# First queries and keys of three attention branches made in the gate stage and placed from SBUF

## The chip, the cores and the metric

One NeuronCore of a Trainium2 chip runs the whole kernel in one launch. The metric is the device time of that launch in microseconds. The engines are TensorE (PE, matmuls and transposes), VectorE (DVE), ScalarE (ACT), GpSimd (POOL) and SyncE (SP, which here only issues DMAs). Each works its own list in order; semaphores order them against each other.

## What is computed

A decoder layer on 1024 tokens of width 1024, in float32. Four causal attention branches work on one input projection; what the change touches is the order of their parts.

```python
def token_mixer(x, w_in, b_forget, sinks, w_branch, w_gate, b_gate, w_out):
    (aq, ak, av, bq, bk, bv, cq, ck, cv, ciq, cik, ciw, dq, dk, dv, df) = split(x @ w_in)
    o_a = banded_attention(aq, ak, av, slopes_a, 127, 1, sinks)     # 8 heads on 2 key heads
    o_b = dilated_attention(bq, bk, bv, slopes_b)                   # 8 heads
    o_c = dsa_attention(cq, ck, cv, ciq, cik, ciw, slopes_c, 256)   # 8 heads on 1 key head, 256 best keys
    o_d = forgetting_attention(dq, dk, dv, df + b_forget)           # 8 heads
    proj = einsum('bsnk,nkd->bsnd', stack(o_a, o_b, o_c, o_d), w_branch)
    gates = sigmoid(x @ w_gate + b_gate)
    return sum(gates * proj, axis=2) @ w_out

def reference(...):
    x = layer_norm(ALPHA * x + token_mixer(x, ...))
    return layer_norm(ALPHA * x + conv_glu_ffn(x, ...))
```

In branch C each query sees the 256 keys of highest index score; where scores are equal, the earlier keys win.

## The kernel before

Every float32 product is made of three matmuls: operands are split into a high part (rounded to a format that TensorE takes at full rate) and a low part (the rest), and hi x hi, lo x hi and hi x lo are summed. ScalarE writes the high part, GpSimd (of weights) or VectorE (of activations) the low part. The list of steps is: transposes of x, the index projections, the index scores, the **gate stage**, then for each branch in the order B, D, A, C: its first q and k projection, its v projection, attention in four pairs of heads, and the **merge** (branch projection and gating), and last the output projection and the feed-forward part.

Gate stage (`GATE_PRODUCTS`, L1225). Of the 32 gate tiles of 128 channels, 22 are made here, two per round, in 11 rounds (`NGATE`). A round takes seven products of 2x2 blocks (of 12 matmuls each) where two plain projections take 96 matmuls. ScalarE and GpSimd make the operands, VectorE combines the products, ScalarE applies the sigmoid, and SP stores the tiles in DRAM (`gates_dram`). Between them VectorE works at the search for the 256th best score of each query (`topk_search`, L2399; 191 steps, up to 14 a round).

Between branches (steps `q`, `k` or `kv_c`). PE runs whole projections of 48 matmuls (L911) into a PSUM pair; ScalarE (`q_hi`, `k_hi`, L1675) and VectorE (`q_lo` L2519, `k_lo` through `lo_part` L2648) place them in `heads`, from PSUM: queries scaled, with the low part below the high one; keys twice, on both halves of the partitions. `heads[:, 0:4]` also holds the operand of the merge before (`o_hi`). Then PE starts v; after 30 matmuls it makes the first scores (L972, L973), and it goes on to the filler (the next pair's projections, L927) only after VectorE has copied v out of PSUM (L2889). In branch C, v comes by transposes of the k/v projection (L963). `biased` (L2504) adds the distance bias and takes the row minimum, ScalarE makes the exponentials (L1777), VectorE the reciprocals (L2514), GpSimd the normalised probabilities (L2230).

Merge. PE makes eight tiles of 24 matmuls (L1247 to L1271) in four PSUM places; `gated` on VectorE (L2957) multiplies each by its gate, and in D and A a second operation (L2962) adds it to the running sum. Tile t+4 waits for the gating of tile t. ScalarE and GpSimd split the next weights meanwhile (L1652, L2175), two tiles ahead; the last of these splits waits for the merge's last tile, and both engines do it before they go on to the next branch. Of B's merge, four tiles of the sum are spilled to DRAM and come back later (`spill`).

Equal scores (`topk_distances`, L2441 to L2456): per 128 queries six steps on VectorE, 36 in all, which turn scores into distances. They and the last steps of the search run beside the merges and the projections between branches (`topk_parts`).

SP issues all loads of weights in the order of the steps, two raw tiles deep. Before branch D it also loads the forget biases of heads 0 and 1 (`forget_bias`, L1511) over the tiles that hold B's bias and the distances. It waits there for the semaphore `bias_used`, which VectorE raises once B's bias and its own use of these tiles are done. `forget_bias(0)` and `(1)` stand right after the load of D's v weights, and the weights of D's second pair behind them.

## Time and profile before

| | us |
|---|---|
| median of 3 runs (lowest, highest) | 2093.43 (2091.26, 2094.61) |
| the profiled execution | 2093.97 |
| its span, first to last instruction | 2092.2 |
| PE busy | 2060.4 (98%) |
| DVE busy | 1536.4 (73%) |
| ACT busy | 968.5 (46%) |
| POOL busy | 937.3 (45%) |

In a profile a group is named by line, engine and operation, then what it writes and reads (`out<-in`) by the program's names. "Idle before" is the time for which the engine stood before the instruction, with what ended it behind an arrow. Matmuls overlap in the records: one of 512 columns is shown with 0.39 us, but the next starts 0.23 us after it. So the distance of starts counts, and PE shown as busy is not PE without loss. A timeline gives start, duration, engine, line and operation; rows in sequence are merged with their count.

### The profile page before, as it was taken

What the parts mean: (1) busy time and instruction counts of PE and PEld (TensorE: products, weight loads), DVE (VectorE), ACT (ScalarE), POOL (GpSimd) and SP (SyncE); (2) the same over time, 40 slices, a digit from 0 to 9 for tenths busy, and PEclk for the clock granted to TensorE, in tenths of its full rate; (3) what the DMA queues carried; (4) which work ended last, traced back from release to release, by engine and by line L of the source; (5) the groups of instructions that cost most, each with busy time, mean ns of one, the idle gap of its engine ahead of it and who ended that gap; (6) DMA issues with size and microseconds to landing.
All of it is one profiled execution on the core that took longest, in us unless ns stands there. A gap on an engine that the chain in (4) does not pass through costs nothing.

```text
span 2092.2 us, 28999 instructions
## 1 busy us (share of the span) xinstructions
PE 2060.4 (98%) x10382; PEld 1727.0 (83%) x10382; DVE 1536.4 (73%) x2549; ACT 968.5 (46%) x1740; POOL 937.3 (45%) x796
## 2 busy tenths in 40 slices
PE   9999999999999999999999999999999999999998
PEld 7788888888888888888888888888788888888887
DVE  8678887777686666797785666668877777775668
ACT  5543334566615556615635666523433333344540
POOL 4287752333322223324523333524756565645651
PEclk9999999999999999999999999999999999999999
DMA  4233323110042111230031000441566665558862
GB/s 132 72 111 110 101 91 62 31 31 21 26 152 64 50 32 51 75 100 28 22 121 31 21 21 11 141 161 61 180 181 203 191 192 161 171 189 310 270 215 92
DMA packets 197373, 224.26 MB, mean 107 GB/s; under 512 B 25704, under 2 KB 149608, under 8 KB 197232
## 3 DMA queue, kind: packets, MB, share of 16 engines
q1 hardware_dynamic: 194320, 212.43, 32.7%
q10 hardware_dynamic: 2912, 10.00, 1.3%
q8 instruction: 83, 1.36, 0.3%
q14 instruction: 58, 0.48, 0.1%
HBM read 164.17 MB, written 58.23 MB: 106 GB/s over the span
## 4 chain that ended last, share of the span: by engine, by line
PE 87%; DVE 7%; issue 2%; ACT 2%; POOL 1%; DMA 0%; DVEq 0%; ACTq 0%; POOLq 0%
PE pair L1359 13%; PE pair L927 13%; PE pair L911 7%; PE pair L1225 7%; PE obank L1359 5%; PE pair L1388 5%; PE obank L1021 4%; PE chunk L1000 4%; PE pair L1318 3%; PE chunk L1388 3%; PE obank L1225 3%; PE pair L972 3%; PE pair L973 3%; PE pair L1271 2%; PE obank L1388 2%
## 5 line engine op out<-in xcount | busy, mean ns | idle before, releaser
L2175 POOL TENSOR_TENSOR w_lo<-w_raw,w_hi 128x1024 fp32r<-128x1024 f32 x64 | 159.5, 2492 | 311.1 <-ACT w_hi L1652 311.0
L1675 ACT ACTIVATE pt_hi<-chunk 128x512 fp32r<-128x512 f32 (+1 forms) x272 | 150.8, 555 | 179.2 <-PE chunk L1000 177.8
L2578 DVE TENSOR_TENSOR pt_lo<-chunk,pt_hi 128x512 fp32r<-128x512 f32 (+1 forms) x272 | 173.2, 638 | 80.1 <-ACT pt_hi L1675 75.7
L2230 POOL TENSOR_SCALAR prob<-prob,att 128x256 f32<-128x256 f32 (+4 forms) x172 | 118.1, 696 | 198.5 <-DVE att L2514 198.2
L927 PE MATMUL pair<-act_hi,w_hi 128*128 128x512 f32 x432 | 186.4, 432 | 2.5 <-DVE heads L2519 2.3
L927 PE MATMUL pair<-act_hi,w_lo 128*128 128x512 f32 x432 | 170.0, 393 | 0.0
L927 PE MATMUL pair<-act_lo,w_hi 128*128 128x512 f32 x432 | 169.4, 392 | 0.0
L2399 DVE TENSOR_SCALAR_CACHE_REDUCE o_top<-score,stat 128x384 uint8<-128x384 f32 (+1 forms) x186 | 167.0, 941 | 0.5
L1021 PE MATMUL obank<-pt_hi,heads 128*128 128x256 f32 (+1 forms) x568 | 148.4, 285 | 0.6 <-DVE pt_lo L2578 0.6
L1777 ACT ACTIVATE prob<-prob,att 128x257 f32<-128x257 f32 (+6 forms) x172 | 120.5, 702 | 39.3 <-DVE att L2504 38.0
L1021 PE MATMUL obank<-pt_lo,heads 128*128 128x256 f32 (+1 forms) x568 | 138.6, 281 | 0.0
L972 PE MATMUL pair<-heads 128*128 128x512 f32 (+3 forms) x352 | 119.9, 347 | 5.7 <-DVE att L2504 4.8
L911 PE MATMUL pair<-act_hi,w_hi 128*128 128x512 f32 x288 | 116.8, 405 | 5.0 <-DVE act_lo L2648 2.7
L1652 ACT ACTIVATE w_hi<-w_raw 128x1024 fp32r<-128x1024 f32 x64 | 67.4, 1053 | 111.8 <-PE obank L1271 38.3
L1000 PE MATMUL chunk<-ident,prob 128*128 128x128 f32 x660 | 111.9, 274 | 2.7 <-DVE pt_lo L2578 2.1
L1021 PEld LDWEIGHTS obank<-pt_lo,heads 128*128 128x128 f32 x568 | 108.2, 190 | 6.8
L1021 PEld LDWEIGHTS obank<-pt_hi,heads 128*128 128x128 f32 x568 | 107.4, 189 | 7.7 <-DVE pt_lo L2578 1.1
L973 PE MATMUL pair<-heads 128*128 128x512 f32 (+3 forms) x352 | 113.1, 334 | 0.0
L911 PE MATMUL pair<-act_lo,w_hi 128*128 128x512 f32 x288 | 112.6, 391 | 0.0
L911 PE MATMUL pair<-act_hi,w_lo 128*128 128x512 f32 x288 | 111.0, 392 | 0.0
L2230 POOL TENSOR_SCALAR mid<-mid,att 128x384 f32<-128x384 f32 (+4 forms) x56 | 37.8, 683 | 162.4 <-DVE att L2514 162.4
L927 PEld LDWEIGHTS pair<-act_hi,w_lo 128*128 128x128 f32 x432 | 81.1, 188 | 18.6
(489 smaller groups left out, 5932.5 us busy)
## 6 DMA issues: line engine op xcount, KB each, us to landing
down_sums<-dn_sums SPq DMA_DIRECT2D x40, 512.0 KB, 6.4
w_raw<-in_w_in SPq DMA_DIRECT2D x37, 512.0 KB, 3.8
gates<-o_t SPq DMA_DIRECT2D x22, 512.0 KB, 2.9
up_raw<-in_w_up SPq DMA_DIRECT2D x22, 512.0 KB, 4.8
gate_raw<-in_w_ffn_gate SPq DMA_DIRECT2D x22, 512.0 KB, 6.0
hidden<-gelu_s SPq DMA_DIRECT2D x22, 512.0 KB, 3.3
dn_raw<-down_sums SPq DMA_DIRECT2D x44, 256.0 KB, 4.1
h_in<-down_sums SPq DMA_DIRECT2D x44, 256.0 KB, 4.8
```

The costliest lines, as they stand in the source:

```text
L911: last = nc.tensor.matmul(dst[0:cols, s:s + HALF], w[:, k, :], a[:, k, s:s + HALF], start=(i == 0), stop=(i == len(order) - 1))
L927: last = nc.tensor.matmul(pair[1][:, s:s + HALF], w[:, k, :], a[:, k, s:s + HALF], start=(k == 0 and n == 0), stop=(k == NKT - 1 and n == 2))
L972: nc.tensor.matmul(dst[:, s:s + m], q, k_hi[:, s:s + m], start=True, stop=False)
L973: last = nc.tensor.matmul(dst[:, s:s + m], q, k_lo[:, s:s + m], start=False, stop=not masked)
L1000: last = nc.tensor.transpose(t[:, at:at + P], prob_slot(br, 2 * j + w)[:, s:s + P], ident[:])
L1021: last = nc.tensor.matmul(obank[bank_of(br)[j] % 2][:, q0:q0 + width], v, part[:, slot, at:at + width], start=(c == 0 and b == 0 and w == ...
L1225: last = nc.tensor.matmul(place, w[:, tokens_of(k)], gate_tokens(p, part, k), start=(p in (1, 6, 5) and k == 0 and m == 0), stop=(k == 3 a ...
L1359: last = nc.tensor.matmul(dst, w[:, cols], moving, start=(p in (1, 6, 5) and k == 0 and m == 0), stop=(k == 3 and m == 2), skip_group_chec ...
L1388: last = nc.tensor.matmul(banks[t], l[:, t * P:(t + 1) * P], r, start=(p in (6, 1, 5, 3) and k == 0 and m == 0), stop=(k == KFF - 1 and m ...
L2175: nc.gpsimd.tensor_tensor(split_into(1, g), w_raw[:, g % 2, 0:kt * cols], split_into(0, g).bitcast(F32), ALU.subtract).then_inc(lo_ready, 1)
L2399: nc.vector.tensor_scalar(junk[:, b % 2, 0:(i + 1) * P], s, limit if isinstance(limit, float) else limit[:, b:b + 1], None, ALU.is_ge, ALU ...
L2578: nc.vector.tensor_tensor(pt_lo[:, n % PT_SLOTS, 0:m], t[:, 0:m], pt_hi[:, n % PT_SLOTS, 0:m].bitcast(F32), ALU.subtract).then_inc(chunk_f ...
```

## The change

The first q and k of branches D, A and C (in C the shared k/v) are no longer projected between branches. They are six more tiles of the gate stage, which grows from 11 to 14 rounds; ScalarE writes them with a copy in place of the sigmoid, and SP stores them in DRAM (`heads_dram`). SP loads them during the merge before the branch into `o_t[:, 0]` and `o_t[:, 1]`, once tile 4 of that merge is free to be gated (`load_heads`). A new step `heads` places them from there in parts, counted by `first_placed`: the first half of the first head, the second half, and the other head. On VectorE the gating of the merge's last tile moves behind the first of these parts; ScalarE spills B's last tile behind the second. The search is now done within the gate stage. Of the equal-score steps, four rows of blocks run beside B's merge, four steps a tile, before the signal `bias_used`; the other two rows run beside D's merge.

```diff
+HEAD_TILES = [(what, br) for br in BRANCH_ORDER[1:] for what in ("q", "k")]
+GATE_TILES = [(br, dt) for br in BRANCH_ORDER for dt in STORED_GATES[br] if (br, dt) not in FILLER_GATES] + HEAD_TILES
...
-        if br == C:
-            out += [("kv_c",)]
-        if br == A:
-            out += [("k", A, 0)]
-        out += [("q", br, 0)]
-        if br in (B, D):
-            out += [("k", br, 0)]
+        out += [("q", br, 0), ("k", br, 0)] if br == B else [("heads", br)]
         out += [("v_c",)] if br == C else [("v", br, 0)]
...
+                    if step[1] != B:
+                        pe.wait_ge(first_placed, placed_first(step[1], 1))
                     scores(step[1], step[2], 0)
...
+            def load_heads(br):
+
+                at = BRANCH_ORDER.index(br) - 1
+                if at == 0:
+                    sp.wait_ge(merge_free, 4)
+                else:
+                    sp.wait_ge(sum_done, sums_of(BRANCH_ORDER[at]) + 4)
+                for what in ("q", "k"):
+                    tile = GATE_TILES.index((what, br))
+                    sp.wait_ge(gate_stored[tile % 2], 16 * (tile // 2 + 1))
+                    sp.dma_start(first_head(what), tile_kept((what, br))).then_inc(heads_loaded, 16)
...
+            def first_heads(br):                                   # ScalarE
+
+                at = BRANCH_ORDER.index(br)
+                act.wait_ge(merge_full, NKT * at)
+                act.wait_ge(heads_loaded, 32 * at)
+                first_half(br, 0)
...
+            def other_heads(br):
+
+                first_half(br, 1)
+                if br == D:
+                    act.wait_ge(merge_free, merge_at(B) + NKT)
+                    spill(NKT - 1)
+                q_hi(br, 0, 1, first_head("q")[HD:P, :])
+                if br != C:
+                    k_hi(1, first_head("k")[HD:P, :])
...
+            def first_half(br, s):                                 # VectorE
+
+                q_lo(br, 0, 0, first_head("q")[0:HD, half_cols(s)], half_cols(s))
+                k_lo(0, first_head("k")[0:HD, half_cols(s)], cols=half_cols(s)).then_inc(first_placed, 1)
+
+            def first_heads(br):
+
+                before = BRANCH_ORDER[BRANCH_ORDER.index(br) - 1]
+                first_half(br, 0)
+                gated(before, NKT - 1)
+                dve.wait_ge(merge_free, merge_at(before) + NKT)
+                if before != B:
+                    dve.wait_ge(sum_done, sums_of(before) + NKT)
...
                 elif kind == "v":
+                    if step[1] != B:
+                        first_half(step[1], 1)
+                    biased(step[1], step[2], 0)
+                    if step[1] != B:
+                        other_head(step[1])
+                    biased(step[1], step[2], 1)
+                    inverse(step[1], 0)
                     if step[1] == D:
                         dve.wait_ge(mid_stored, 16 * len(SPILLED))
-                    if step[1] == A:
-                        topk_parts((SEARCH_PARTS - topk_done.n) % DISTANCE_PARTS)
-                    for u in range(2):
-                        biased(step[1], step[2], u)
-                    inverse(step[1], 0)
...
                 if (br, pr) == (C, 0):
                     biased(br, pr, 0)
                     biased(br, pr, 1)
+                    first_half(br, 1)
+                    other_head(br)
                     inverse(br, 0)
...
-                    topk_parts(start_parts)
-                    for dt in range(NKT):
+                    if br == D:
+                        topk_parts(LATE_DISTANCES)
+                    elif br == A:
+                        own(nc.vector.tensor_copy(dist_a[:], dist[:, SEQ - 2 * P:SEQ]))
+                    for dt in range(NKT if br == FINAL else NKT - 1):
...
+                        if br == B and dt < ROWS_BESIDE:
+                            topk_parts(EARLY_ROWS * DISTANCE_PARTS // ROWS_BESIDE)
+                            if dt == ROWS_BESIDE - 1:
+                                signal().then_inc(bias_used, 2)
```

The two engines' own marks behind `def first_heads` and `def first_half` are added here for the reader.

## Rows read from the trace of the kernel before

**Rows 1.** The page's first part: busy time of PE.
```profile
PE 2060.4 (98%) x10382; PEld 1727.0 (83%) x10382; DVE 1536.4 (73%) x2549; ACT 968.5 (46%) x1740; POOL 937.3 (45%) x796
```

**Rows 2.** Busy us (count): PE, PEld, DVE, ACT, POOL; gate stage, B's merge.
```profile
105.00:314.00 209.00, 209.00 (x923) 173.06 (x923) 178.30 (x426) 77.82 (x121) 151.09 (x118) 1.00 0.34 104
...
572.00:615.00 43.00, 43.00 (x191) 35.45 (x191) 36.00 (x71) 9.10 (x10) 9.65 (x4) 1.00 0.56 183
```

**Rows 3.** Timeline of PE: merge ends, and starts of what waits.
```profile
615.41 0.39 PE L911 MATMUL pair<-act_hi,w_hi 128*128 128x512 f32 x1
...
650.93 0.50 PE L927 MATMUL pair<-act_hi,w_hi 128*128 128x512 f32 x1
...
920.68 0.39 PE L911 MATMUL pair<-act_hi,w_hi 128*128 128x512 f32 x1
...
955.29 0.49 PE L927 MATMUL pair<-act_hi,w_hi 128*128 128x512 f32 x1
...
1098.10 0.39 PE L911 MATMUL pair<-act_hi,w_hi 128*128 128x512 f32 x1
...
1127.39 0.50 PE L972 MATMUL pair<-heads 128*128 128x512 f32 x1 [0.76 <-DVE att L2504]
```

**Rows 4.** Timelines of DVE, ACT and POOL at the end of B's merge.
```profile
615.68 1.23 DVE L2957 TENSOR_TENSOR mid<-obank,prob 128x1024 f32<-128x1024 f32 x1 [0.69 <-PE obank L1271]
...
615.67 1.06 ACT L1652 ACTIVATE w_hi<-w_raw 128x1024 fp32r<-128x1024 f32 x1 [9.82 <-PE obank L1271]
...
616.81 2.41 POOL L2175 TENSOR_TENSOR w_lo<-w_raw,w_hi 128x1024 fp32r<-128x1024 f32 x1 [8.48 <-ACT w_hi L1652]
```

**Rows 5.** Placement of half heads (timelines), of whole ones from SBUF (tile heads).
```profile
668.78 1.38 DVE L2648 SCALAR_TENSOR_TENSOR heads<-pair,heads 64x512 fp32r<-64x512 f32 x2 [0.80 <-ACT heads L1675]
...
667.49 1.19 ACT L1675 ACTIVATE heads<-pair 64x512 fp32r<-64x512 f32 x2
...
L2648 DVE SCALAR_TENSOR_TENSOR heads<-mid,heads x12: 1216/1220/1223, 398.0 to 827.8; 64x1024 fp32r<-64x1024 f32 x12
```

**Rows 6.** Timelines of DVE and POOL: sums at the end of D's merge.
```profile
917.50 1.22 DVE L2962 SCALAR_TENSOR_TENSOR mid<-mid,prob 128x1024 f32<-128x1024 f32 x1
...
922.31 3.25 DVE L2962 SCALAR_TENSOR_TENSOR mid<-mid,prob 128x1024 f32<-128x1024 f32 x1
...
922.08 2.40 POOL L2175 TENSOR_TENSOR w_lo<-w_raw,w_hi 128x1024 fp32r<-128x1024 f32 x1 [8.48 <-ACT w_hi L1652]
```

**Rows 7.** Timelines of ACT and DVE at first scores, D and C.
```profile
648.66 0.51 ACT L1777 ACTIVATE prob<-prob,att 128x256 f32<-128x256 f32 x1 [2.59 <-DVE att L2504]
...
649.65 1.23 DVE L2889 COPY mid<-pair 128x1024 f32<-128x1024 f32 x1 [0.18 <-PE pair L911]
...
1123.70 0.76 DVE L2648 SCALAR_TENSOR_TENSOR heads<-chunk,heads 128x256 fp32r<-128x256 f32 x2
1124.49 0.29 DVE L2504 CUSTOM_DVE_ANT_0 prob<-pair,dist_a 128x128 f32<-128x128 f32 x1
...
1126.18 0.54 DVE L2504 CUSTOM_DVE_ANT_0 aux<-pair,score 128x384 f32<-128x384 f32 x1
```

**Rows 8.** SP: timeline, waits by cause (570 to 640), DMA issues (626 to 627).
```profile
625.34 0.81 SPq L1511 DMA_DIRECT2D aux<-c_forget  x2
626.19 6.20 SPq L1410 DMA_DIRECT2D w_raw<-in_w_in  x2
...
SPq L1510 <- DVE stat L2356: 16.5, 1, 16.5
...
w_raw<-in_w_in SPq DMA_DIRECT2D x1, 512.0 KB, 6.1
```

**Rows 9.** Timeline of DVE: gating of B's tile 5, equal-score steps of 768.
```profile
604.80 1.23 DVE L2957 TENSOR_TENSOR mid<-chunk,o_t 128x1024 f32<-128x1024 f32 x1 [0.69 <-PE chunk L1271]
...
930.07 1.76 DVE L2448 TENSOR_TENSOR_SCAN aux<-prob 128x768 f32<-128x768 f32 x1
931.86 1.02 DVE L2452 SCALAR_TENSOR_TENSOR prob<-aux,stat,prob 128x768 f32<-128x768 f32 x1
```

More of the change, by code:

```diff
@@ L794, in gate_bias_of, with tile_weights, tile_kept, first_head @@
             return gate_bias[:, br * NKT + dt:br * NKT + dt + 1]
+        def tile_weights(tile):
+            if tile not in HEAD_TILES:
+                return w_tile(w_gate[0], tile[0] * D_MODEL + tile[1] * P, P)
+            what, br = tile
+            return w_tile(w_in[0], Q_COL[br] if what == "q" else CK if br == C else K_COL[br], P)
+        def tile_kept(tile):
+            return heads_dram[HEAD_TILES.index(tile)] if tile in HEAD_TILES else gates_dram[tile]
+        def first_head(what):
+            return o_t[:, 0 if what == "q" else 1, :]
+        def placed_first(br, part):
+            return 3 * (BRANCH_ORDER.index(br) - 1) + part
         gate_out = [o_t[:, 2, :], o_t[:, 3, :]]
@@ L1518, in _ @@
                                  allow_slow_non_contiguous=True).then_inc(late_params, 16)
+                if step[0] == "heads":
+                    load_heads(step[1])
                 for n, source in enumerate(ring_sources(step)):
@@ L2795, in _ @@
                     dve.wait_ge(consts_ready, 1)
-                if kind == "kv_c":
-                    topk_parts(10 ** 6)
-                    own(nc.vector.tensor_copy(dist_a[:], dist[:, SEQ - 2 * P:SEQ]))
                 if kind == "x":
@@ L2832, in _ @@
                         counted(9)
-                    topk_parts(TOPK_FIRST.get(step[:2], 0))
-                    if step == ("q", D, 0):
-                        dve.wait_ge(pair_free[0], tiles[0].n)
-                        signal().then_inc(bias_used, 2)
                     k = step[1] in (B, D)
```

200 lines of the change are left out of this document (102 added, 98 removed).

## The prediction, made before the change was run

> **What bounds the kernel now.** I read the page first: TensorE (PE) is busy for 2060.4 of 2092.2 us [rows 1]. Then I read the stretches by stage: in the gate stage PE is busy for all 209.00 us while it starts 923 matmuls, which makes 0.2264 us a matmul of 512 columns; VectorE (DVE) has 178.30 us of work there, and in the merge of branch B 36.00 of 43 us [rows 2]. So PE sets the end as long as its operands arrive, and a change is worth what it takes from PE's list less what PE then has to wait. Last I read the three places where one branch ends and the next begins. The reader is to see there where PE starts the first removed projection, and where it starts the work that can't begin before the vector engine has caught up [rows 3].
>
> The profiled execution took 2093.97 us (span 2092.2), the median of the three runs is 2093.43. I make the sum against 2093.97 and take off the half microsecond at the end.
>
> **What PE loses and gains in work.** Six projections go from between the branches: q and k of D, k and q of A, the shared k/v and q of C. Each is 8 k-tiles x 2 halves x 3 parts = 48 matmuls, together 288, or 65.3 us at 0.2267 us (209.4 us over the stage's own 924). Three rounds come to the gate stage, each 7 products x 12 = 84 matmuls, together 252, or 57.1 us. The rounds there so far leave PE no idle time [rows 2]; VectorE does 14 search steps a round there before and after, so I give the new rounds the same pace. All search steps (14 rounds x 14 - 2 = 194 places for 191 steps) now fit in the stage; before, 39 of them ran between the branches, beside PE work that covered them, so taking them from there gives PE nothing. Net: **-8.2 us**.
>
> **What covered the turn from branch to branch, and no longer does.** At each turn 96 matmuls, 21.8 us of PE work, disappear. Under them VectorE did its last gating, ScalarE (ACT) and VectorE placed q and k, and ScalarE split the next weights. Now PE has only the v projection (or, in the turn to C, eight transposes and 12 matmuls) while all of this follows in one chain after the merge's last matmul. Let e be that end: VectorE and ScalarE start within 0.1 us of it, so e is 615.6 for B to D, 920.9 for D to A, 1098.3 for A to C [rows 3, 4].
>
> The chain, from rows: ScalarE first splits a weight tile (1.06 us), and GpSimd (POOL) starts its 2.4 us low part at e+1.2 [rows 4]. ScalarE then places the first half of one head: three activations of 64x512, two of which took 1.19 [rows 5]; the first is there at about e+1.75. VectorE's partner ops (half width 0.69 each, full width 1.22 [rows 5]) read their source from SBUF now, and the subtracted part too, where the removed ones read PSUM. The nearest rows say what that means beside GpSimd: the same kind of op with both inputs in SBUF took 1.22 us alone and 3.25 when GpSimd had begun a 2.40 us split just before; it ended 1.1 us after GpSimd did [rows 6]. So VectorE's first placement waits for e+3.6. The bounds are e+1.75 (no blocking) and e+3.6; I take the latter, since the conditions are those of the slow row.
>
> The Trainium skill, page SBUF — State Buffer, section "Who interferes with whom", has this as a rule: a VectorE instruction with two SBUF inputs contends with a GpSimd instruction that reads SBUF, and whoever starts first has the shared ports for the whole instruction. The row of 3.25 us agrees. By the rule and by the row the wait is the same 1.85 us at each turn; it speaks against reading the first heads from SBUF.
>
> **D to A.** VectorE: three half ops to e+5.7; the gating of the last tile and its sum, 1.2 each, to e+8.2; second half of the first head to e+10.3; the first scores' softmax start 0.4; the other head, three full ops, to e+14.4; the second start 0.5; exp 0.6 and reciprocal 0.2; copy of v 1.23 [rows 7], to e+17.1. PE's filler can't begin before this copy, as before, where it began at 955.29 right behind it. Before, less the 21.8 us removed, is 933.5; now 938.05. **Loss 4.5 us.** GpSimd's six tiny sink ops and two bias ops may add up to 1 us by the same ports.
>
> **B to D.** The same chain without the sum, with shorter score ops: copy done and filler begun at e+15.65 = 631.3 against 650.93 - 21.77 = 629.2, a loss of 2.1. The last tile's spill (an issue from ScalarE's queue, moved behind the second half of the first head) costs nothing: the second head's VectorE ops come later anyhow. But here a moved step has a second effect. SyncE (SP), after the v weights, waits for bias_used before it sends two loads of forget biases, and only behind them the next weights (k of the second pair). Those are the very tile that ScalarE now splits at e, ahead of every placement; before, that place had k of the first pair, loaded long ago. SyncE stands in this wait for 16.5 us in the trace, and its weight load, sent behind the two bias loads, landed 6.1 us after its issue [rows 8]. The signal now comes after VectorE's steps beside tile 5 of merge B. Tile 5 is gated from 604.8 for 1.2 us; then four steps of the 768-wide row, 1.76 + three of about 1.02 [rows 9], make 610.8, and 613.0 if the scan meets GpSimd's split. Add 0.85 to the issue and 6.1 to the landing [rows 8]: the weights are there at 620.0, 4.3 us after ScalarE wanted them; without the port effect 618. PE, which wants the first placed heads 30 matmuls (6.8 us) into v, then stands. **Loss 2.1 + 4.3 = 6.4 us**, bounds 0.2 and 8.
>
> **A to C.** PE's cover is 1 us of transposes and 2.7 of filler. VectorE: first half to e+5.7, gating and sum to e+8.2, v's low parts 0.76, two score ops 0.65 (0.29 and a wider one) [rows 7], second half 2.1, other q 1.2, reciprocal, two more score ops 1.15 (0.54 in the row and the next wider), to e+14.2. Unit 4 of the scores waits for these, as it did at 1127.39. Now 1112.5 against 1127.39 - 21.77 = 1105.6. **Loss 6.9 us**, bounds 5.0 (no blocking) and 8.
>
> **Edits at nothing.** The copies in place of sigmoids for the six tiles take the same slot on ScalarE. Six stores of 512 KB go out in the gate stage as the 22 others do, six loads come during merges with some 20 us to land. The equal-score steps in merge B just fit: the 768-wide row's six steps are those 4.8 us and two of about 0.8, and the rows of 384, 512 and 640 scaled from it bring the four to some 20 us, with 7.3 for six gatings, in the 32.6 us that PE takes for six tiles; PE's v needs the gating of tile 6 done, by my sum at 614.3 against 615.4; should they be late by 2 us, 1 us is lost. Five steps at merge D's start run before the first tile is ready or delay it within PE's four places.
>
> **Sum.** -8.2 + 6.4 + 4.5 + 6.9 = +9.6 us: 2103.6, against the median 2103.1.
>
> **Rivals.**
> The forget-bias wait is hidden (the steps finish early, or the load lands faster): B to D loses 2.1 only, sum +5.3, 2099.3. Against it: the loads in order behind one another [rows 8].
> GpSimd doesn't block (it splits later, or VectorE gets in first): the turns cost 2.7 + 2.7 + 5.0, sum +2.2, 2096.2; with the bias wait gone too, 0.2 + 2.7 + 5.0 - 8.2, 2093.7: **no change**. This decides from losses under 12.4 us on. For it speaks that only one kind of op is seen blocked; against it the start times.
> **Faster**: the placement runs under v, and PE keeps its saving: 2085.8 at most. It decides where the three losses stay under 4 us together. For it: PE's waits on placement are small today. Against: my shortest chain for C alone loses 5.
> Worse than forecast: more port conflicts and merge B's steps late, 2107 to 2109.
> That the change doesn't do what it says: the new gate rounds stretch to VectorE's pace. It is busy 85% there; I leave this in the worse case.
>
> **How the numbers follow.** Forecast 0.45, hidden bias wait 0.15, worse 0.05: slower 0.65. No blocking, with or without the bias wait: 0.20. Faster 0.15. Bounds of 0.2% (4.2 us) are about what a measurement of this kernel can tell from no change. The range has its upper end from C and B to D at 8 and A at 5.5 (+13.3, 2107), its lower end 2091, so that it takes in all of no change and leaves most of faster out.
>
> **What the profile will show.** PE's idle time: some 6 us before unit 4 of C, up to 4 us before the first placed scores of D and more before the first transposes of probabilities in D and A. Placement ops on VectorE of 2 us and more at each turn where GpSimd runs. A weight split on ScalarE at 620, not 615.7, of the turn to D (all moved by 57 us), released by a DMA. The gate stage 266.5 us long without a gap. I'm wrong if PE shows under 4 us of waits at the three turns together, or if PE's losses sit in the gate stage.

## The result, and the profile after

The changed kernel took 2113.46 us, the median of five runs (2112.66 to 2114.48), against 2093.43 before: a ratio of 1.0097, with a 95% interval of 1.0082 to 1.0111. It is slower by 20 us. The forecast was slower, but at 2103.1, with a range that ended at 2107: the direction was right and the size half of what came. All medians here are of executions at nearly full clock (0.99 and more); one execution of one kernel below, e8_spread, took 3782.84 us at a granted clock of 0.80 and is left out.

The profiled execution of the changed kernel took 2112.66 us (span 2110.8), 18.7 more than that of before. The page's first line on PE answers [rows 1]: fewer matmuls and less busy time, in a longer span. So the time is in PE's waits and not in its work.

```profile
span 2110.8 us, 29071 instructions
PE 2058.3 (98%) x10346; PEld 1724.3 (82%) x10346; DVE 1547.6 (73%) x2572; ACT 983.0 (47%) x1776; POOL 962.9 (46%) x823
```

The next view answers [rows 2]: busy time and count of PE, PEld, DVE, ACT and POOL, then the granted clock and the DMA share, in the gate stage (some 57 us longer than before), and in the merge of B.

```profile
105.00:371.30 266.30, 266.30 (x1176) 220.50 (x1176) 228.10 (x545) 98.18 (x154) 193.19 (x151) 1.00 0.35 106
...
630.00:673.00 43.00, 42.77 (x189) 34.96 (x187) 38.00 (x47) 8.29 (x9) 10.31 (x4) 1.00 0.53 183
```

PE is busy for all of the gate stage. To see where the rest went, the timeline of PE is read at the edges of the merges, here of the changed kernel: first matmul of merge B and of merge D, first matmuls behind merge D, first of merge A, first work behind merge A, first of the last merge.

```profile
628.97 0.44 PE L1264 MATMUL pair<-heads,w_hi 128*128 128x512 f32 x1
...
924.27 0.45 PE L1264 MATMUL pair<-heads,w_hi 128*128 128x512 f32 x1
...
969.79 0.39 PE L925 MATMUL pair<-act_lo,w_hi 128*128 128x512 f32 x1
...
1088.16 0.44 PE L1264 MATMUL pair<-heads,w_hi 128*128 128x512 f32 x1
...
1132.13 0.38 PE L977 MATMUL chunk<-ident,o_t 128*128 128x128 f32 x2
...
1330.57 0.45 PE L1264 MATMUL pair<-heads,w_hi 128*128 128x512 f32 x1
```

In the table a stretch runs from one such edge to the next (the last matmul of a merge where it says end). "Due" is the stretch before, less the 21.77 us of projections that left it; the loss is what the changed kernel took beyond that.

| stretch | before | due | after | loss | predicted |
|---|---|---|---|---|---|
| up to the start of merge B | 571.78 | 628.9 (+57.1) | 628.97 | 0.1 | 0 |
| start of merge B to start of D's | 304.93 | 283.16 | 295.31 | 12.15 | 6.4 |
| merge D | 43.75 | 43.75 | 45.06 | 1.31 | 0 |
| end of merge D to start of A's | 133.69 | 111.92 | 118.83 | 6.91 | 4.5 |
| end of merge A to start of the last | 213.62 | 191.85 | 198.67 | 6.82 | 6.9 |
| the rest | 780.68 | 780.68 | 780.21 | -0.5 | 0 |

Merge A takes 43.73 us in both. Added up: 57.2 - 65.3 + 12.15 + 1.31 + 6.91 + 6.82 - 0.5 = +18.6 us, the difference of the two spans. The three turns lose 25.9 us where 17.8 were forecast, and merge D loses 1.3 that were not.

What PE waited for, by cause (total, times, longest), first at the turn to D (670 to 700), then from merge D over the turn to A (924 to 1000), then at the turn to C (1131 to 1150):

```profile
PE pair L986 <- DVE heads L2705: 5.6, 1, 5.6
PE pair L925 <- DVE mid L2858: 3.2, 1, 3.2
PE chunk L1014 <- POOL prob L2282: 0.8, 1, 0.8
...
PE pair L986 <- DVE att L2559: 3.7, 1, 3.7
PE pair L1288 <- issue: 1.4, 1, 1.4
PE chunk L1014 <- POOL prob L2282: 1.0, 1, 1.0
...
PE pair L986 <- DVE att L2559: 4.8, 2, 2.9
PE pair L986 <- DVE heads L2705: 2.0, 1, 2.0
```

The waits at the turn to C make 6.8 us (before the change PE waited 1.2 us there, 0.4 and the 0.76 of [rows 3]). At the turn to D they make 9.6 of 12.15, at the turn to A 4.7 of 6.91. Besides, the granted clock is at half (1.2 of 2.4 GHz) for 6.8 us from 687.8, from 984.8 and from 1138.4. This is the turn to A, 6.8 us at half and the 10 us behind them:

```profile
984.80:991.60 6.80, 5.60 (x17) 4.53 (x18) 2.82 (x9) 2.52 (x8) 1.15 (x4) 0.50 0.00 0
991.60:1001.60 10.00, 10.00 (x63) 8.81 (x63) 6.02 (x21) 4.99 (x16) 3.77 (x13) 1.00 0.00 0
```

What the half clock costs depends on where it lies. While VectorE works through its chain, a slower PE only waits less afterwards. So each turn is divided where PE can't go on before VectorE has caught up: at the start of the filler in D and A, at the scores of unit 4 in C (1146.69, below). VectorE's copy of v in D, and the first filler matmul of D and of A:

```profile
697.20 1.22 DVE L2980 COPY mid<-pair 128x1024 f32<-128x1024 f32 x1
...
698.56 0.47 PE L941 MATMUL pair<-act_hi,w_hi 128*128 128x512 f32 x1
...
987.35 0.78 PE L941 MATMUL pair<-act_hi,w_hi 128*128 128x512 f32 x1
```

Measured from the last matmul of the merge, with 21.77 us taken off before, the turns to D, A and C lose 12.2, 4.9 and 7.0 us up to this point, and -0.1, 2.0 and -0.2 us behind it. In D and C the half clock ends ahead of this point. VectorE works there with no gap of more than 0.1 us, from 684.75 to 696.4 and from 1134.0 to 1146.5, so the half clock costs nothing. In A it goes on for 4.3 us behind the filler's start, where PE has no wait that it didn't have before, and it is what the 2.0 us are.

**The turn to D.** In merge B, VectorE never stands still after the first tile, and it is late. Its timeline (starts, durations), with GpSimd's three splits of that stretch behind it:

```profile
639.51 1.27 DVE L2454 TENSOR_SCALAR_CACHE_REDUCE o_top<-score,stat 128x1024 uint8<-128x1024 f32 x1
...
643.72 2.56 DVE L2505 SCALAR_TENSOR_TENSOR prob<-aux,stat,prob 128x384 f32<-128x384 f32 x1
...
654.16 2.76 DVE L2511 SCALAR_TENSOR_TENSOR score<-prob,aux 128x512 f32<-128x512 f32 x1
...
666.40 2.01 DVE L2499 TENSOR_SCALAR prob<-score,stat 128x768 f32<-128x768 f32 x1
...
674.57 0.06 DVE L2411 MEMSET stat<- 128x1 f32 x1
674.64 1.23 DVE L2858 TENSOR_TENSOR mid<-pair,prob 128x1024 f32<-128x1024 f32 x1
...
643.30 2.57 POOL L2227 TENSOR_TENSOR w_lo<-w_raw,w_hi 128x1024 fp32r<-128x1024 f32 x1 [3.54 <-ACT w_hi L1677]
...
653.45 2.93 POOL L2227 TENSOR_TENSOR w_lo<-w_raw,w_hi 128x1024 fp32r<-128x1024 f32 x1 [7.58 <-ACT w_hi L1677]
...
665.59 2.40 POOL L2227 TENSOR_TENSOR w_lo<-w_raw,w_hi 128x1024 fp32r<-128x1024 f32 x1 [9.21 <-ACT w_hi L1677]
```

The row of 639.51 is the last step of the search, which still stands in merge B: with its short followers it takes 1.9 us. The next three rows are steps that began while GpSimd was at a split: 2.0, 2.1 and 1.4 us longer than steps of about their size elsewhere in the merge (0.61 with 384 columns, 0.56 and 0.82 with 384 and 640, 0.56 with 640). (The third has one input in SBUF, not two; the Trainium skill, page SBUF — State Buffer, section "Who interferes with whom", says that a tensor_scalar can enter a mode in which it uses the shared ports as well, and the row agrees. I had weighed only the rule for two inputs.) So the signal bias_used comes at 674.57 (forecast: 670.2), and tile 6 is gated at 675.87. PE, whose v projection needs that, starts at 675.92. The weights that ScalarE wants were sent at 675.54 and are there at 683.1, 10.5 us after the merge's end (forecast: 4.4). From then on the chain runs as forecast: split, blocked placement, first scores.

```profile
683.14 1.06 ACT L1677 ACTIVATE w_hi<-w_raw 128x1024 fp32r<-128x1024 f32 x1 [17.63 <-DMA w_raw<-in_w_in]
...
684.75 2.42 DVE L2574 SCALAR_TENSOR_TENSOR heads<-o_t,heads 64x512 fp32r<-64x512 f32 x1 [8.88 <-ACT heads L1700]
...
688.62 0.47 PE L986 MATMUL pair<-heads 128*128 128x128 f32 x1 [5.61 <-DVE heads L2705]
```

PE's wait for tile 6 adds nothing to this: had PE begun v at once, it would have waited that much longer for the first placed heads.

**Merge D.** The five steps at its start do harm, in the other direction: the scan started 0.15 us before GpSimd's split, the split took 1.6 us longer than its usual 2.4, and PE had to wait for its weights.

```profile
932.52 2.02 DVE L2501 TENSOR_TENSOR_SCAN aux<-prob 128x896 f32<-128x896 f32 x1
932.67 4.03 POOL L2227 TENSOR_TENSOR w_lo<-w_raw,w_hi 128x1024 fp32r<-128x1024 f32 x1 [11.45 <-ACT w_hi L1677]
...
936.80 0.70 PE L1288 MATMUL pair<-heads,w_hi 128*128 128x512 f32 x2 [1.41 <-issue]
```

**The turns to A and to C.** VectorE's first placement of A is blocked (2.40 us instead of 0.69), and PE then waits for the second softmax start, which stands behind the other head. In C there are three waits, for the placed heads and for softmax starts.

```profile
971.50 2.40 DVE L2574 SCALAR_TENSOR_TENSOR heads<-o_t,heads 64x512 fp32r<-64x512 f32 x1 [0.48 <-ACT heads L1700]
...
985.03 0.58 PE L986 MATMUL pair<-heads 128*128 128x256 f32 x1 [3.70 <-DVE att L2559]
...
1137.92 0.33 PE L986 MATMUL pair<-heads 128*128 128x128 f32 x1 [2.03 <-DVE heads L2705]
...
1141.62 0.69 PE L986 MATMUL pair<-heads 128*128 128x384 f32 x1 [2.87 <-DVE att L2559]
...
1146.69 0.47 PE L986 MATMUL pair<-heads 128*128 128x512 f32 x1 [1.93 <-DVE att L2559]
```

### The profile page after: what moved, and what is told of

Same layout as the page of the kernel before. It is cut to its first block, busy times and chain, and to the rows that moved or that the text cites. A ratio compares the mean times of both kernels' runs of the same rounds, so it can differ in the third digit from the quotient of the medians.

```text
span 2110.8 us, 29071 instructions
## 1 busy us (share of the span) xinstructions
PE 2058.3 (98%) x10346; PEld 1724.3 (82%) x10346; DVE 1547.6 (73%) x2572; ACT 983.0 (47%) x1776; POOL 962.9 (46%) x823
## 4 chain that ended last, share of the span: by engine, by line
PE 82%; DVE 10%; issue 3%; ACT 2%; DMA 2%; POOL 1%; ACTq 0%; DVEq 0%; SPq 0%
PE pair L1376 13%; PE pair L941 13%; PE pair L1242 9%; PE obank L1376 5%; PE obank L1035 4%; PE chunk L1014 4%; PE pair L1405 4%; PE obank L1242 4%; PE pair L925 4%; PE pair L1335 3%; PE pair L986 3%; PE pair L987 2%; PE pair L1288 2%; PE chunk L1405 2%; PE obank L1405 2%
## 5 line engine op out<-in xcount | busy, mean ns | idle before, releaser
L2227 POOL TENSOR_TENSOR w_lo<-w_raw,w_hi 128x1024 fp32r<-128x1024 f32 x58 | 146.4, 2524 | 271.6 <-ACT w_hi L1677 271.6
L941 PE MATMUL pair<-act_hi,w_hi 128*128 128x512 f32 x432 | 187.4, 434 | 2.5 <-DVE heads L2574 2.3
L941 PE MATMUL pair<-act_hi,w_lo 128*128 128x512 f32 x432 | 170.7, 395 | 0.0
L941 PE MATMUL pair<-act_lo,w_hi 128*128 128x512 f32 x432 | 170.2, 394 | 0.0
L1677 ACT ACTIVATE w_hi<-w_raw 128x1024 fp32r<-128x1024 f32 x58 | 61.1, 1053 | 123.7 <-DMA w_raw<-in_w_in 52.1
L1376 PE MATMUL pair<-t,op_late 128*128 128x512 f32 x396 | 95.5, 390 | 1.0 <-POOL op_late L2237 0.7
L986 PEld LDWEIGHTS pair<-heads 128*128 128x128 f32 x352 | 67.4, 191 | 35.3 <-DVE att L2559 15.1
L1376 PE MATMUL pair<-t,op_early 128*128 128x512 f32 x396 | 95.1, 389 | 0.1
```

The source lines that it names most:

```text
L941: last = nc.tensor.matmul(pair[1][:, s:s + HALF], w[:, k, :], a[:, k, s:s + HALF], start=(k == 0 and n == 0), stop=(k == NKT - 1 and n == 2))
L986: nc.tensor.matmul(dst[:, s:s + m], q, k_hi[:, s:s + m], start=True, stop=False)
L1376: last = nc.tensor.matmul(dst, w[:, cols], moving, start=(p in (1, 6, 5) and k == 0 and m == 0), stop=(k == 3 and m == 2), skip_group_chec ...
```

## The experiments

My theory after the result: the turn to D is held by two things that come from VectorE's late steps in merge B (tile 6, and the weights behind the forget biases); A and C by the row of vector work with a blocked placement at its head; and half clock comes on top (by the division above it costs time in A alone). The rivals: vector lateness alone, the port lock alone, or a want of PE work beside the chains. "Port lock" is short for what the slow rows show: of the two engines' instructions, the one that started second took about as much longer as the other still had to run. All kernels are edits of the changed kernel and share its lines but for a few. Their losses are read from the edges of the merges, as above (turn to D, merge D, turn to A, turn to C; changed kernel: 12.15, 1.31, 6.91, 6.82).

### One order altered in SyncE's queue

```diff
-                if step == ("v", D, 0):
-                    forget_bias(0)
-                    forget_bias(1)
+                    if n == 1 and step == ("attn", D, 0):   # behind the first weights of D's pairs
+                        forget_bias(0)
+                        forget_bias(1)
```

> The changed kernel with one order altered: SyncE sends the load of k's weights of the second pair of D ahead of its wait for bias_used and the two forget-bias loads, instead of behind them. Theory (the turn from B to D is held by this weight tile, which ScalarE splits ahead of every placement): ScalarE splits at about 673, not 683.1; the copy of v ends near 689, not 698.4; the stretch from merge B to merge D loses some 4 us instead of 12.2, and the time falls by about 8 us, to 2105. Rival 1 (the vector engine's late steps in merge B hold the turn by themselves): PE still starts v at 675.9 and the first placed scores stay near 688; gain under 2 us, 2112. Rival 2 (a delay of the forget-bias loads behind the weights takes its place): gain about 4.

Measured: 2109.09 us (ratio to before 1.0076, 1.0061 to 1.0091). The turn to D loses 5.51 instead of 12.15; merge D 1.27, A 6.59, C 8.17. ScalarE splits at 673.0, and the copy of v is at 690.75. Of the 6.6 us gained, 1.35 are given back at C, where nothing was edited: the half clock lay in two other pieces there, and the second (from 1141.05) stood behind the start of unit 4 (1139.85). What is left at the turn to D is PE's wait for tile 6, with VectorE idle later for 3 us until PE brings the first scores:

```profile
673.03 1.06 ACT L1677 ACTIVATE w_hi<-w_raw 128x1024 fp32r<-128x1024 f32 x1 [7.03 <-PE obank L1288]
...
676.40 0.50 PE L925 MATMUL pair<-act_hi,w_hi 128*128 128x512 f32 x1 [3.46 <-DVE mid L2858]
```

So the weights behind the forget biases were real. With them out of the way the late steps show as a second cause, which stood in their shadow before.

### Fewer steps beside merge B

To this the next kernel adds three rows of equal-score steps beside merge B, instead of four:

```diff
-EARLY_ROWS = 4
-LATE_DISTANCES = 5
+EARLY_ROWS = 3
+LATE_DISTANCES = 4
```

> The changed kernel with the weights ahead of the forget biases, as in e1_weights_first, and with three rows of equal-score steps (18 steps) beside merge B instead of four (24); the fourth row's six go to merge D (4 steps at its start, 14 beside its tiles). Theory (what e1_weights_first left of the B to D loss, 3.5 us of PE's wait for the gating of tile 6 and 1.7 us of half clock behind it, comes from the vector steps of merge B): PE starts v without a wait, B to D loses 1 us or less instead of 5.5, time 4 to 4.5 us below e1_weights_first, 2104.7. Rival 1 (merge D can't take six more steps): the turn to A loses 3 us more, 2108. Rival 2 (the wait for tile 6 isn't from the number of steps): nothing changes against e1_weights_first, 2109.

Measured: 2106.47 us (1.0069, 1.0053 to 1.0086). The turn to D loses 1.92; merge D 0.82; but A 9.12; C 6.85. The wait for tile 6 of merge B is gone, so it came from the number of steps; and rival 1 holds as well: it stands again at the next merge, as one wait of 6.0 us.

```profile
PE pair L925 <- DVE prob L2858: 6.0, 1, 6.0
```

### The split behind the placing

```diff
                     else:
-                        ahead()            # at the end of a merge
 ...
                 if br != C:
                     k_hi(1, first_head("k")[HD:P, :])
+                ahead()                    # behind both heads
```

> The changed kernel with one ScalarE step moved at each of the three turns: the split of the next weight tile stands behind the placing of both heads, not ahead of it; GpSimd's low part follows it there. Theory (split and port lock stand at the head of the chain): the first placement on VectorE takes 0.7 us, not 2.4, and starts 1.06 us earlier at A and C; D no longer waits for the DMA. D turn gains 8 to 9 us, A 2.9, C 2 to 2.9: time 2099 to 2101. Rival 1 (the lock only moves: another VectorE op with two inputs in SBUF takes 2 us more beside GpSimd's split): 1.9 us of it comes back at A and at C, 2103. Rival 2 (A and C are bound by the row of VectorE ops alone, the split costs nothing): only D gains, 2105.

Measured: 2109.30 us (1.0079, 1.0064 to 1.0094). Turn to D 7.05, merge D 1.3, A 6.42, C 8.28. The placement at the head of each chain takes 0.69 us, as the theory said, and D's placing no longer waits for the DMA, but D keeps its wait for tile 6 (3.5 us), with half clock for 6.8 us. And A gains 0.5 only: GpSimd now splits ahead of making A's biases, and the first softmax start waits for those. In C GpSimd's split meets the second half of the first head. Rows of A and C:

```profile
966.18 0.69 DVE L2573 SCALAR_TENSOR_TENSOR heads<-o_t,heads 64x512 fp32r<-64x512 f32 x1
...
976.18 0.35 DVE L2558 CUSTOM_DVE_ANT_0 prob<-pair,o_t,sink_neg 128x128 f32<-128x128 f32 x1 [2.67 <-POOL o_t L2321]
...
1134.88 1.98 DVE L2573 SCALAR_TENSOR_TENSOR heads<-o_t,heads 64x512 fp32r<-64x512 f32 x1
```

Rival 1 is what happened: the lock moved.

### The other head behind the copy of v

The vector engine's three full-width placements go behind the copy of v (A and D) and behind the softmax starts of units 2 and 3 (C):

```diff
                     biased(step[1], step[2], 0)
-                    if step[1] != B:
-                        other_head(step[1])
                     biased(step[1], step[2], 1)
                     inverse(step[1], 0)
 ...
                     nc.vector.tensor_copy(stage(step[1]), src[:, :]).then_inc(pair_free[1], 1)
+                    if step[1] != B:
+                        other_head(step[1])
```

> The changed kernel with VectorE's three full-width placements of the other head moved: in D and A behind the copy of v, in C behind the softmax starts of units 2 and 3. Nothing else is altered. Theory (PE waits for whatever stands behind these 3.7 us in VectorE's order): A's wait of 3.7 us and with it the stretch at half clock go, 5 to 6 us; D gains 3.7; C gains 2 (the waits ahead of scores 4); together 10 to 12 us, 2102 to 2104. Rival (the placements are wanted just as soon: the first P^T low parts come late instead): each turn gains under 1 us, 2111 or more.

Measured: 2112.51 us (1.0093, 1.0078 to 1.0108). Turn to D 16.2, merge D 1.3, A 3.42, C 5.73. A's wait of 3.7 us went, with the half clock behind it, and a new one of 2.3 came, for the low part of P^T that the placements now hold up; D, where the copy was late anyway, lost 4 us more. Up to the filler's start it lost 12.1, as in the changed kernel; behind it came a wait of 2.6 us for the low part of P^T, and the last of three pieces of half clock (3.4 us from 706.1). Theory at A, in part at C, rival at D; by the time the rival held.

```profile
993.96 0.66 PE L977 MATMUL chunk<-ident,prob 128*128 128x128 f32 x4 [2.33 <-DVE pt_lo L2633]
```

### The other head later still

The same placements at the end of group 0 (A and D) or 1 (C), behind the low parts of P^T and v; where they stood, VectorE now only counts ScalarE's parts for them.

```diff
                     for what, h in placed(br, pr, g):
                         place(br, pr + 1, what, h)
+                    if br != B and pr == 0 and g == (1 if br == C else 0):
+                        other_head(br)
```

> The changed kernel with VectorE's placements of the other head moved further than in e3_head_behind: behind the first low part of P^T and the low parts of v, at the end of group 0 (A and D) or 1 (C); ScalarE's order is untouched. Theory (in A they stood ahead of the second softmax start, in e3_head_behind ahead of the first P^T low part; behind both nothing waits for them): D to A loses under 1 us instead of 6.9, C 1 to 2 less, D nothing less since its weights come late anyway: 2105 to 2106. Rival (unit 8 of A, asked two groups on, now waits for them): half of it comes back, 2109.

Measured: 2112.75 us (1.0095, 1.0078 to 1.0110). Turn to D 14.44, merge D 1.29, A 3.18, C 6.88. A keeps what the kernel before this won and no more; C gains nothing, though the scores of its unit 4 start 1.3 us earlier behind the merge's end (13.3 instead of 14.6 us): six us on, the moved placement (1.22 us, at 1149.86) stands ahead of another softmax start, PE waits 0.86 us for it, and the scores behind it start 21.8 us after the merge's end, as before (22.0). D again is worse: up to the filler's start it loses 10.9, but behind it 3.5 more, where PE waits 2.0 us for the probabilities of GpSimd and the last of three pieces of half clock (3.4 us from 706.7) stands. By the time even the rival (2109) was too low.

### More cover ahead of C

24 instead of 12 filler matmuls stand ahead of C's first scores; the 12 are taken from groups 6 to 11:

```diff
-FIRST_C = 4
+FIRST_C = 8
-BESIDE_C = (((0, 0), (0, 2), ..., (3, 1), (6, 0), (6, 2), (8, 1), (10, 1), (11, 2), (12, 2), ...
+BESIDE_C = (((0, 0), (0, 2), ..., (3, 1), (6, 0), (12, 2), ...
```

> The changed kernel with 24 instead of 12 filler matmuls ahead of the first scores of C; the 12 are taken from groups 6 to 11 of the same stream. PE's work is the same. Theory (the turn to C is lost for want of PE work beside the chain): 2.7 us more cover take the 2.0 us wait for the first placed heads and 0.7 of the next; 2110.7, or 2109.5 if the half clock goes as well. Rival (the filler is missed where it was): 2113.4, with new waits in groups 6 to 11.

Measured: 2113.65 us (1.0100, 1.0085 to 1.0115); C loses 8.19, of which 1.3 us lie behind the start of unit 4, as in e1_weights_first and with the half clock in the same two places. The wait for the first placed heads is gone, and the scores of unit 4 start 14.6 us after the merge's end, as without the cover. The waits of P^T for its low parts rose from 1.6 to 3.6 us (10 instead of 6). The rival held: C's pace up to there is VectorE's, and cover only moves PE's waits.

### Steps of merge D spread

```diff
                     if br == D:
-                        topk_parts(LATE_DISTANCES)
+                        pass
 ...
-                            topk_parts(((NSC - EARLY_ROWS) * DISTANCE_PARTS - LATE_DISTANCES) // (NKT - 1))
+                            left = (NSC - EARLY_ROWS) * DISTANCE_PARTS
+                            topk_parts(left * (dt + 1) // (NKT - 1) - left * dt // (NKT - 1))
```

> The changed kernel with no equal-score step ahead of merge D's first tile; all twelve stand beside its tiles 0 to 6. Theory (a 2.0 us scan of the five steps at the start holds up GpSimd's weight split, 4.0 us instead of 2.4, and PE waits 1.4 us for it): that wait goes, 2112.1. Rival (the steps beside the tiles come late for the last gating): merge D gains 1.4, the turn to A loses as much or more.

Measured: 2114.55 us, the median of three (1.0105, 1.0088 to 1.0122), no gain. Its rows can't be set beside the others, so they don't tell where the time went: the theory's 1.4 us in the time didn't come, and whether the turn to A took them, as the rival says, stays open. The next kernel has the same spreading, and its merge D takes 43.41 us, 1.65 less than in the changed kernel: the wait of 1.4 us is gone there.

### Steps beside three merges

Weights ahead of the forget biases; 18 steps beside merge B, 12 spread over merge D, one beside each of the first six tiles of merge A.

```diff
+                        elif br == A and dt < ROWS_OF_A:      # 6
+                            topk_parts(1)
```

> The changed kernel with the weights ahead of the forget biases and the 36 equal-score steps put at 18 beside merge B, 12 beside merge D (none ahead of its first tile) and 6 beside merge A. Theory (each merge has vector time for 12 to 18 steps, and what is late in a merge is a wait at the next turn): B to D as in e5_first_three_rows (285.1 us from merge to merge), D to A without its 6.0 us wait for tile 6, 162.5, A to C as in the changed kernel, 242.4: together 11.5 us less, 2102. Rival (the six steps in merge A come late for its last tiles): A to C 2 to 3 us more, 2104.5.

Measured: 2105.98 us (1.0062, 1.0047 to 1.0077). Turn to D 4.71, merge D -0.34, A 7.92, C 9.42. The wait of 6.0 us at A is gone, no wait for tile 6 is left at any turn. The turn to C loses 2.6 us more, the rival's figure, but not by its cause: PE's waits there are those of e5_first_three_rows (2.0, 3.0 and 1.9 us), with half clock for 13.7 us instead of 6.8. So the sum is 4 us short of the theory, and the next view shows the same at the turn to D. This kernel and e5_first_three_rows are the same program up to merge D. Their turns to D in two windows each (15 and 7 us; PE's busy time and count first, the granted clock third from the end), first e5_first_three_rows, then e10_rows_three_ways:

```profile
672.00:687.00 15.00, 13.48 (x64) 10.90 (x62) 11.52 (x14) 9.85 (x15) 2.40 (x1) 1.00 0.40 131
687.00:694.00 7.00, 6.04 (x35) 4.95 (x34) 4.41 (x11) 3.04 (x9) 0.83 (x2) 1.00 0.00 0
```

```profile
672.00:687.00 15.00, 13.47 (x64) 10.81 (x62) 11.61 (x15) 9.96 (x15) 2.40 (x1) 1.00 0.41 131
687.00:694.00 7.00, 6.06 (x20) 4.86 (x19) 3.56 (x8) 2.38 (x6) 0.82 (x2) 0.52 0.00 0
```

The same work and the same wait (1.5 us) in the first 15 us, a second wait of 0.9 us in both right behind, and then full clock in one and half clock for 6.8 us in the other: 35 matmuls against 20. The stretch from merge B to merge D is 2.79 us longer in the second (287.87 against 285.08), 2.5 of them behind the filler's start.

### Dummy matmuls in the waits

Matmuls whose result nobody reads, first 12 in the wait of A, then 15 there and 8, 10 and 7 in the three waits of C:

```diff
                     for _part in tile:
                         pass
+                    if step[1] == A:
+                        pe.wait_ge(merge_free, merge_tiles.n)
+                        for k in range(12):
+                            nc.tensor.matmul(obank[1], act_hi[:, 0, 0:P], act_hi[:, 0, 0:HALF], start=True, stop=True)
```

> The changed kernel with 12 matmuls of 128x512 added on PE between the v projection of A and the scores behind it, in PE's wait; their result is read by nobody. They are 2.7 us of work in a wait of 3.7. Theory (PE's idle time there lets the granted clock fall to half from 984.8 to 991.6, which costs 2.4 us beyond the wait): the clock stays full, merge A starts 2.4 us earlier, 2111.0. Rival 1 (the clock falls for another reason): it falls all the same and nothing is gained, 2113.4. Rival 2 (the added work gets in the way): slower by up to 2.7 us.

> The changed kernel with PE's waits at the turns to A and to C filled by matmuls of 128x512 whose result nobody reads: 15 in the wait of 3.7 us in A, 8, 10 and 7 ahead of the scores of units 0, 2 and 4 in C. Theory (idle PE lets its clock fall, and the fall costs what of it lies outside the waits): the half clock of 6.8 us after the turn to A goes and D to A is 2.4 us shorter; in C the half clock goes too, but there it lay in the waits, so nothing is gained: 2111. Rival (the clock falls at a turn for another reason than idle PE): half clock as before, 2113.4 or more.

Measured: 2113.41 us (1.0094, 1.0078 to 1.0111) with the 12, 2112.92 (1.0095, 1.0080 to 1.0110) with all. With 12, A loses 6.23 and half clock there lasts 3.4 instead of 6.8 us; with 15, A loses 6.33 and it lasts 3.4 us too, now from 989.1. At C, in e9_busy_turns, it is gone, and the loss is 6.73, as before. The clock's column there, e9_busy_turns first, then the changed kernel:

```profile
1130.00:1150.00 20.00, 17.52 (x84) 13.65 (x83) 13.68 (x24) 11.22 (x22) 4.08 (x5) 1.00 0.09 27
```

```profile
1131.00:1150.00 19.00, 12.17 (x55) 9.15 (x54) 14.18 (x25) 11.21 (x22) 4.49 (x5) 0.82 0.10 28
```

So at C the half clock cost nothing in the changed kernel, since it lay beside VectorE's chain and in the waits for it, and the loss is that chain's alone. At A a piece of it came although PE had been given work and with the 15 had only waits of 0.3 and 1.3 us left; halving it won 0.6 to 0.7 us there, and nothing clear in the time. That it is idle time of PE which lets the clock fall is borne out at C, where it went with the waits filled (in one execution), and left open at A.

### The cures together

Rows beside three merges and weights first, with the other head late in A and C (and where it was in D):

```diff
+                    if br in (A, C) and pr == 0 and g == (1 if br == C else 0):
+                        other_head(br)
```

> As e10_rows_three_ways, with VectorE's placement of the other head late (behind group 0) in A, behind group 1 in C, and where it was in D. Theory (losses of the turns are separate and add up): 3.7 us less in D to A, 1.3 in A to C: 2097 to 2098. Rival (in C the row of vector work up to group 6 sets the pace, whatever its order): C gains nothing, 2098.5. Rival 2 (the savings at one turn are given back at the next): 2101.

Measured: 2103.08 us (1.0050, 1.0033 to 1.0067). Turn to D 5.11, merge D -0.35, A 3.85, C 8.40, with half clock for 10.2 us at the turn to C. A gains 4.1 against the kernel without the late head, in part because no half clock stood at that turn this time. C gains nothing that could be told from the clock. The time is 2 us above the highest that was expected.

To this, the split behind the placing, and GpSimd's split in A behind its biases and sinks:

```diff
+                    if step[0] != "heads":
+                        split_weights(min(needed + (1 if step[0] == "v" else 2), len(ring_list)) - ring.n)
-                    split_weights(min(needed + (1 if step[0] == "v" else 2), len(ring_list)) - ring.n)
                     if step == ("heads", A):
```

> As e11_together, with ScalarE's split of the next weights behind the placing of both heads, and GpSimd's low part behind its biases and sinks in A. Theory (the split and the port lock at the head of each chain cost 2.9 us where the chain of vector work binds): D to A 2 us less, A to C 1 us less, B to D unchanged: 2094.5. Rival (GpSimd's split moved behind meets other two-input steps of VectorE and gives 1.9 us back at each turn): 2097.5, as e11_together.

Measured: 2100.36 us (1.0036, 1.0023 to 1.0049). Turn to D 4.45, merge D -0.3, A 3.77, C 7.45: above the rival's 2097.5 too. In the profiles D gains 0.7 us, A 0.1 and C 0.95, with less half clock at D and C (3.4 us instead of 6.8, 6.8 instead of 10.2), and the part behind the turns, which no edit touches, 1.2; so what the moved split won can't be told from these. The first placements at C and the next there show that the lock moved once more, within one chain:

```profile
1120.30 0.68 DVE L2575 SCALAR_TENSOR_TENSOR heads<-o_t,heads 64x512 fp32r<-64x512 f32 x1 [3.11 <-ACT heads L1700]
...
1127.01 1.96 DVE L2575 SCALAR_TENSOR_TENSOR heads<-o_t,heads 64x512 fp32r<-64x512 f32 x1
```

13 of the 20 us are back, and no kernel beats the one before. Nor is there much to hope for: a branch whose two projections move saves 21.77 - 19.03 = 2.74 us, and the smallest losses seen in any of the kernels are 1.9 us at D, 3.2 at A and 5.7 at C. Only D's smallest loss lies below the saving; no run moved D's projections alone.

## Why the prediction was right in direction and half in size

**The work.** Right to 0.1 us. The gate stage has no gap and is 57.1 us longer; PE loses 8.2 us of work, net.

**The chain and the port lock.** Right. The first placement took 2.42, 2.40 and 2.47 us at the three turns. In A the copy of v ended 17.15 us after the merge's end, forecast 17.1; in D it was 15.3 us after the split began, forecast 15.65. With the split moved away, the placement took 0.69. What was too simple is the price of the lock: taken from the head of the chain, the lock came back on another step of it (1.96 us in C), or GpSimd's own work came late (2.67 us in A). In one kernel it was worth 0.5 us at A, not 1.9.

**The forget-bias wait.** Right in mechanism: the experiment that alters only that order wins 6.6 us at the turn, and ScalarE's split shows its release by a DMA. Of its terms, bias_used came 4.4 us later than in my sum, and the landing took 7.6 us instead of 6.1 (with another weight load sent right behind it; no run shows whether that is why). So the weights were there 5.9 us later than forecast, and this is all that the sum lacks at D: 12.15 lost instead of 6.4.

**The steps in merge B.** This is the first step that failed: "just fit", and the price for being late, 1 us for 2. I had counted the four steps of one row and assumed the tiles before on time. Tile 5 was gated at 668.44 and not at 662.0 (604.8 + 57.2). I counted no port lock in a merge in which three weight splits run beside two dozen vector steps (5.4 us), and took the last search step to fit in the gate stage (1.9 us). The signal for the forget biases was 4.4 us late by it, and PE's v waited 3.2 us, which cost nothing only because the weights came later still. With the weights sent ahead and 18 steps instead of 24 both went: 1.92 us were left at the turn. No run has the 18 steps with the weights where they were.

**Merge D.** "Run before the first tile is ready or delay it within PE's four places" was wrong. I asked what the steps do to the gating, not what they do to GpSimd: the lock has two sides, and the weight split waited for a scan. 1.3 us.

**D to A.** The chain was right to 0.1 us up to the copy of v and to 0.4 up to the filler (4.9 us lost, forecast 4.5), and the whole loss was 6.9. The missing term is the clock: no term of my sum allowed for matmuls behind a wait at half rate, though the trace of before has a piece of it (3.4 us at 1028). At A it is 2.0 us, the part of the loss behind the filler's start; with half clock for 3.4 us (e4_clock_fill) 1.3 are left there. At D and C it cost nothing in the changed kernel. The pair of equal programs (e5_first_three_rows and e10_rows_three_ways, the same up to merge D) puts 6.8 us of it, nearly all behind the filler's start, at 2.8 us.

**A to C.** 6.9 forecast, 6.8 measured, with unit 4 at 14.6 us behind the merge's end (forecast: 14.2). Neither more cover nor the filled waits won anything. A piece of half clock behind the start of unit 4 makes it 8.2 (e1_weights_first, e4_clock_fill, e7_cover_c); the forecast had no term for that, and it was luck that the profiled execution of the changed kernel had none there.

So of the losses 9.5 us were missing in the sum: 5.75 at D (the weights, 4.4 us late by the steps in merge B and 1.5 by the landing, less some 0.2 that the rest was quicker), 1.3 in merge D and 2.4 at A (2.0 for the clock). The range was too narrow because its bound of 8 us at D left 1.6 us of room where 5.75 came, and because no bound had room for merge D or the clock. The rival that names the late steps ("more port conflicts and merge B's steps late") had a chance of 0.05 and ended at 2109.

## What to carry to other kernels

Work that is removed from the engine that bounds a kernel may be the cover of a chain on other engines: before it goes, write out that chain op by op from the last event it depends on, and compare its end with what PE has left to do; here 21.8 us of PE work went at each turn and 7 to 12 us were lost again. Steps that move to another engine's "free" time have to be laid against every other queue that shares something with it, in both directions; a late signal is late for every queue that waits for it. And a cure at the head of a chain is only worth what the next link lets through: a turn with several late links pays back in parts.

## What the runs showed of the hardware

**The granted clock after short waits.** PE's clock fell to half for 3.4 or 6.8 us (up to 13.7 in e10_rows_three_ways) at nearly every turn with waits of 1 to 6 us. It isn't reproducible: of two executions with the same work and the same waits (1.5 and 0.9 us) one kept full clock and the other had 6.8 us of half clock and was 2.8 us longer. Where the piece falls decides its price: nothing when it lies beside a chain that PE waits for anyway (D and C in the changed kernel), 2.0 us at A, 2.8 us where nearly all of it stood behind the chain. That puts some 2 us of noise on every comparison of turns above. The turn to C lost 1.35 and 1.4 us more in two kernels that hadn't touched it (e1_weights_first and e4_clock_fill), each with the half clock in two pieces, the second behind the start of unit 4.

**The ports shared by VectorE and GpSimd block either side.** VectorE's placement of 0.69 us took 2.4 when GpSimd's split had started first; GpSimd's split of 2.40 took 4.03 when VectorE's scan had. A tensor_scalar of 768 with one input in SBUF took 2.01 us beside a split, where those of 640 and 896 took 0.56 and 0.69.
